# Big experts in fp32 on 64 and 32 wide column tiles, with 96 slots, one larger ring and experts in plain order

## The reference

```python
logits = (xf @ w_router).astype(jnp.float32)
vals, idx = lax.top_k(logits, TOP_K)
gates = jax.nn.softmax(vals, axis=-1)
combine = jnp.sum(jax.nn.one_hot(idx, N_EXPERTS, dtype=jnp.float32) * gates[..., None], axis=1)
for e in range(N_EXPERTS):
    y = y + combine[:, e:e + 1].astype(xf.dtype) * swiglu(xf, w1[e], w3[e], w2[e])
```

## Time and profile before

| what | value |
|---|---|
| median of 3 runs | 1207.49 us (1205.4 to 1207.52) |
| profiled execution, its own time | 1207.14 us |
| its span, first to last instruction | 1205.3 us |
| TensorE busy | 1149.9 us, 95% |
| VectorE busy | 669.2 us, 56% |
| ScalarE busy | 562.7 us, 47% |
| mean granted TensorE clock | 0.988 |
| moved | 351.08 MB, 291 GB/s over the span |
| weights split for big experts | 216 units on ScalarE (265.3 us) and on VectorE (308.0 us) |

### The profile page before, as it was taken

One profiled execution on the slowest core, in us unless ns is written; L12 is line 12 of the kernel. 1 busy time (PEld: TensorE's weight loads), 2 busy tenths in 40 slices (PEclk: granted clock), 3 DMA queues, 4 the chain that ended last, 5 costly groups with the idle time before them and its releaser, 6 DMA issues.

```text
span 1205.3 us, 16293 instructions
## 1 busy us (share of the span) xinstructions
PE 1149.9 (95%) x6555; PEld 852.7 (71%) x6555; DVE 669.2 (56%) x740; ACT 562.7 (47%) x642; POOL 49.6 (4%) x93
## 2 busy tenths in 40 slices
PE   5989899999999999899999999999999999999995
PEld 5979778888879976685486688648658468387351
DVE  4875664544455523582384788427578058574143
ACT  4772355344444476452363677226447056263131
POOL 8010000000000022000000000000000000000000
PEclk9999999999999999999999999999999999999998
DMA  9632059755325822139999999999999999999992
GB/s 319 184 116 72 29 169 369 238 175 187 128 70 177 330 74 72 66 139 416 413 415 410 413 415 412 400 414 414 411 414 415 415 412 412 413 413 415 413 407 78
DMA packets 116737, 351.08 MB, mean 291 GB/s; under 512 B 8136, under 2 KB 55280, under 8 KB 116656
## 3 DMA queue, kind: packets, MB, share of 16 engines
q1 hardware_dynamic: 115552, 347.11, 74.8%
q0 software_dynamic: 1104, 2.86, 0.8%
HBM read 348.89 MB, written 1.05 MB: 290 GB/s over the span
## 4 chain that ended last, share of the span: by engine, by line
PE 88%; DVE 4%; ACT 2%; DMA 2%; POOL 2%; issue 1%; POOLq 0%; DVEq 0%; ACTq 0%
PE ps L620 20%; PE ps L621 19%; PE ps L622 19%; PE ps L1717 11%; PE ps L1738 7%; PE ps L1661 3%; DMA room<-in_o_moe_w_dram 2%; PE ps L1673 1%; PE ps L1370 1%; DVE low L1904 1%; POOL level L741 1%; PE ps L1578 1%; PE ps L1590 1%; DMA gam<-in_e_sgu_w_dram 1%; PE ps L1698 1%
## 5 line engine op out<-in xcount | busy, mean ns | idle before, releaser
L1904 DVE TENSOR_TENSOR low<-room,all_hi 128x1408 fp32r<-128x1408 f32 (+1 forms) x216 | 308.0, 1458 | 202.6 <-ACT all_hi L883 202.0
L883 ACT ACTIVATE all_hi<-room 128x1408 fp32r<-128x1408 f32 (+1 forms) x216 | 265.3, 1255 | 258.6 <-DMA room<-in_o_moe_w_dram 177.4
L1717 PE MATMUL ps<-room,xg_raw 128*64 128x512 f32 (+1 forms) x768 | 152.5, 558 | 0.0
L620 PE MATMUL ps<-all_hi,xg_hi 128*128 128x512 f32 (+1 forms) x384 | 144.8, 377 | 2.0 <-DVE low L1904 1.0
L621 PE MATMUL ps<-low,xg_hi 128*128 128x512 f32 (+1 forms) x384 | 144.6, 376 | 0.0
L622 PE MATMUL ps<-all_hi,xg_lo 128*128 128x512 f32 (+1 forms) x384 | 144.0, 375 | 0.0
L620 PE MATMUL ps<-all_hi,x_hi 128*128 128x512 f32 (+1 forms) x336 | 125.1, 372 | 5.1 <-ACT xn L972 2.4
L621 PE MATMUL ps<-dense_lo,x_hi 128*128 128x512 f32 (+1 forms) x336 | 122.8, 366 | 0.0
L622 PE MATMUL ps<-all_hi,x_lo 128*128 128x512 f32 (+1 forms) x336 | 122.5, 365 | 0.0
L1717 PEld LDWEIGHTS ps<-room,xg_raw 128*64 128x64 f32 x768 | 54.6, 137 | 95.5 <-issue 95.4
L1897 DVE TENSOR_TENSOR dense_lo<-slots_a,all_hi 128x2048 fp32r<-128x2048 f32 x40 | 91.4, 2290 | 47.5 <-ACT all_hi L876 47.5
(11 more groups left out here) (363 smaller groups left out, 1566.9 us busy)
## 6 DMA issues: line engine op xcount, KB each, us to landing
room<-in_o_moe_w_dram SPq DMA_DIRECT2D x256, 704.0 KB, 15.6
room<-in_o_moe_w_dram SPq DMA_DIRECT2D x80, 1024.0 KB, 18.2
slots_c<-in_e_ffn_w_dram SPq DMA_DIRECT2D x36, 512.0 KB, 6.8
slots_a<-in_e_ffn_w_dram SPq DMA_DIRECT2D x30, 512.0 KB, 5.3
slots_a<-in_e_w_in_dram SPq DMA_DIRECT2D x24, 512.0 KB, 8.7
slots_a<-in_o_w_qkv_dram SPq DMA_DIRECT2D x18, 512.0 KB, 4.5
room<-in_o_moe_w_dram SPq DMA_DIRECT2D x16, 512.0 KB, 17.1
slots_a<-in_e_w_out_dram SPq DMA_DIRECT2D x8, 512.0 KB, 4.0
```

The costliest lines, as they stand in the source:

```text
L620: pe.matmul(o, a_hi, b_hi, start=first, stop=False)
L883: act.activation(unit_hi(st), raw_of(v, off, st.size), ACT.Copy).then_inc(hi_done, 1)
L1717: last = mm(ps[a * SMALL:(a + 1) * SMALL, o + b, 0:n], xg_raw[:, c, :], raw[a][:, c0:c0 + n], start=(c == 0), stop=(c == DC - 1))
L1904: tt(unit_lo(st), raw_of(v, off, st.size), unit_hi(st).bitcast(F32), ALU.subtract).then_inc(lo_done, 1)
```

## The change

1. Big experts no longer split their weights. Their products are plain fp32, with 96 slots instead of 128. The first 64 slots are done on two column tiles of 64, each with a quarter (704 columns, in two parts of 352) of the inner width. The remaining 32 slots are done on four column tiles of 32, with 384, 320, 384 and 320 columns. The down step does the same with 2 x 512 and 4 x 256 columns.
2. The slots lie in more places than before, so the turn, the way back (a second matrix `back_r`), the carrying back (`carry_back`) and the table of remainders (limits of 96, and 128 more behind them) follow the new layout. A remainder would now begin above 96 tokens.
3. The high parts of the dense weights and 11 KB behind the dense ring join the expert ring, which has 147 KB a partition. The two pieces of an up step pair of a big expert share a semaphore.
4. The phases run in plain order: (0, half 0), (0, half 1), (1), (2, half 0), ... The last expert's down phase writes bank 3, not bank 6.
5. ScalarE and VectorE keep the evacuations, SiLU, gate and additions. `xg_lo` and `m_lo` go.

```diff
@@ -41,9 +41,10 @@
     FC = FF // P
     NE = o_router.shape[2]
     CW = 256
-    SLOTS, SMALL = P, 64
-    NB = SEQ // SLOTS
-    NK = NB * NE
+    SLOTS, SMALL, MANY = P, 64, 96
+    LATE = MANY - SMALL
+    NK = 2 * NE + NE // 2
+    assert MANY + SLOTS < SEQ <= MANY + 2 * SLOTS
...
@@ -103,13 +104,19 @@
 
 
     HALF, HB = FF // 2, FC // 2
-    UP_COLS = ((0, 512), (512, 512), (1024, HALF - 1024))
+    QUART, WIDE, NARROW = HALF // 2, 384, 320
+    PAIR_COLS = ((0, 512), (512, 512), (1024, HALF - 1024))
+    MANY_COLS = ((0, QUART // 2), (QUART // 2, QUART // 2), (QUART, WIDE))
+    LATE_COLS = ((0, WIDE), (WIDE, NARROW), (QUART, WIDE), (QUART + WIDE, NARROW))
+    EVEN_BLOCKS = QUART // P
+    M64, M32 = HB * SMALL, (HB + 1) * LATE
+    assert QUART == WIDE + NARROW and QUART - EVEN_BLOCKS * P == SMALL and WIDE == 3 * P and HB == 2 * EVEN_BLOCKS + 1
...
         return q % 2 == 0
 
-    PHASE = [(0, 0), (1, 0), (0, 1)] + [(q, a) for q in range(2, NE) for a in range(2 if big(q) else 1)]
-    ENDING = [1, 0] + list(range(2, NE))
+    PHASE = [(q, a) for q in range(NE) for a in range(2 if big(q) else 1)]
+    ENDING = list(range(NE))
     PHASES = len(PHASE)
     LAST = [max(n for n in range(PHASES) if PHASE[n][0] == q) for q in range(NE)]
...
+            STEPS.append(st)
+
+
+    BEFORE, AFTER = 2 * SPLITS * DC * CW, 2 * HALF
+    ROOM = BEFORE + RING * DC * CW + AFTER
     ARRIVE = 20
...
+                    j, nb = pc.part
+                    both = o_moe_w2[0][bass.ds(e, 1), rows, :].rearrange("e (s r) d -> (e s) r d", s=2)
+                    r0 = j // 2 * P
+                    dst = raw_of(v, 0, pc.size)
+                    if nb == 2:
+                        src = both[:, r0:r0 + P, :].rearrange("s p d -> p s d")
+                        dst = dst.rearrange("p (s d) -> p s d", s=2)
+                    else:
+                        src = both[:, r0:r0 + SMALL, :]
...
-                n = SLOTS if big(q) else SMALL
+                n = MANY if big(q) else SMALL
                 pe.wait_ge(prep_done, TILES * (q + 1))
                 for c in range(DC):
                     for t in range(TILES):
...
                         pe.wait_ge(hTl_ready, TURN0 + 1)
-                    for i, j in enumerate(turn_blocks(b)):
-                        last = pe.transpose(ps[:, turn_bank(n, b), i * P:(i + 1) * P], u_act[:, j * P:(j + 1) * P], ident[:, :])
+                    o = ps[:, turn_bank(n, b), :]
+                    if not big(PHASE[n][0]):
+                        for i, j in enumerate(turn_blocks(b)):
+                            last = pe.transpose(o[:, i * P:(i + 1) * P], u_act[:, j * P:(j + 1) * P], ident[:, :])
+                    elif b == 0:
+                        for i in range(4):
+                            last = pe.transpose(o[:, i * P:(i + 1) * P], u_act[:, i * P:(i + 1) * P], ident[:, :])
+                    elif b == 1:
+                        pe.transpose(o[:, 0:P], u_act[:, 4 * P:5 * P], ident[:, :])
+                        for k in range(2):
+                            half = slice(k * SMALL, (k + 1) * SMALL)
+                            last = mm(o[half, P:P + SMALL], u_act[:, 5 * P:QUART], ident[:, half], start=True, stop=True)
+                    else:
+                        for i in range(3):
+                            pe.transpose(o[:, i * P:(i + 1) * P], u_act[:, QUART + i * P:QUART + (i + 1) * P], ident[:, :])
+                        at = 2 * P + LATE
+                        last = mm(o[SMALL:P, at:at + LATE], u_act[:, QUART + 2 * P:QUART + NARROW], ident[:, 3 * LATE:P],
+                                  start=True, stop=True)
                     last.then_inc(hT_done, 1)
 
...
                     last = pe.transpose(ps[0:SLOTS, bank, t * P:(t + 1) * P], sel_w[:, t, :], ident[:, :])
+                if big(q):
+                    for t in range(TILES):
+                        last = pe.transpose(ps[0:SLOTS, bank, SEQ + t * P:SEQ + (t + 1) * P], sel_r[:, t, :], ident[:, :])
                 last.then_inc(back_done, 1)
+
+            def carry_back(q, t):
+
+                for turn, cols, first in ((back, slice(0, 512), True), (back_r, slice(512, D), False)):
+                    for y in (y_hi, y_lo):
+                        for hf in range(2):
+                            rows = slice(hf * SMALL, (hf + 1) * SMALL)
+                            last = mm(ps[:, SCAT[q][2 * t + hf], :], turn[rows, t, :], y[rows, cols], start=first and y is y_hi,
+                                      stop=not first and y is y_lo)
+                            if not first and y is y_lo:
+                                last.then_inc(scat_done, 1)
 
             def scatter(q, parts=range(4)):
                 k = NTH[q]
...
                 turn = back_last if q == NE - 1 else back
+                if big(q):
+                    for t in sorted({m // 2 for m in parts}):
+                        carry_back(q, t)
+                    return
                 for m in parts:
                     if not big(q) and q < NE - 1 and m:
                         pe.wait_ge(scat_added, 4 * (k - 1) + m)
                     t, hf = m // 2, m % 2
-                    if big(q):
-                        for y, first in ((y_hi, True), (y_lo, False)):
-                            last = mm(ps[:, SCAT[q][m], :], turn[:, t, :], y[:, hf * 512:(hf + 1) * 512], start=first, stop=not first)
-                    else:
-                        rows = slice(hf * SMALL, (hf + 1) * SMALL)
-                        last = mm(ps[:, SCAT[q][m], :], turn[rows, t, :].bitcast(F32), y_small[rows, :], start=True, stop=True)
-                    last.then_inc(scat_done, 1)
+                    rows = slice(hf * SMALL, (hf + 1) * SMALL)
+                    mm(ps[:, SCAT[q][m], :], turn[rows, t, :].bitcast(F32), y_small[rows, :], start=True, stop=True)\
+                        .then_inc(scat_done, 1)
+
+            def arrived(st):
+
+                v, _ = st.pieces[-1]
+                pe.wait_ge(ring_in[arrive_sem(v)], arrive_count(v))
 
...
 
                 (c, w), o = st.part, 3 * st.part[1]
-                if st.big:
-                    pe.wait_ge(lo_done, A_MOE + st.at + 1)
-                    hi, lo = unit_hi(st), unit_lo(st)
-                    for b, (c0, n) in enumerate(UP_COLS):
-                        last = product(pe, ps[:, o + b, 0:n], xg_hi[:, c, :], xg_lo[:, c, :], hi[:, c0:c0 + n], lo[:, c0:c0 + n],
-                                       c == 0, c == DC - 1)
-                    last.then_inc(piece_used, 1)
-                    return
-                for v, _ in st.pieces:
-                    pe.wait_ge(ring_in[arrive_sem(v)], arrive_count(v))
+                first, end = c == 0, c == DC - 1
+                arrived(st)
                 raw = [raw_of(v, 0, HALF) for v, _ in st.pieces]
-                for b, (c0, n) in enumerate(UP_COLS):
-                    for a in range(2):
-                        last = mm(ps[a * SMALL:(a + 1) * SMALL, o + b, 0:n], xg_raw[:, c, :], raw[a][:, c0:c0 + n],
-                                  start=(c == 0), stop=(c == DC - 1))
+                if big(st.q):
+                    for b, (c0, n) in enumerate(MANY_COLS[0:2]):
+                        for a in range(2):
+                            mm(ps[a * SMALL:(a + 1) * SMALL, o + b, 0:n], xg_many[:, c, 0:SMALL],
+                               raw[0][:, a * QUART + c0:a * QUART + c0 + n], start=first, stop=end)
+                    for a, (c0, n) in enumerate(LATE_COLS):
+                        last = mm(ps[a * LATE:(a + 1) * LATE, o + 2, 0:n], xg_many[:, c, SMALL:MANY], raw[0][:, c0:c0 + n],
+                                  start=first, stop=end)
+                else:
+                    for b, (c0, n) in enumerate(PAIR_COLS):
+                        for a in range(2):
+                            last = mm(ps[a * SMALL:(a + 1) * SMALL, o + b, 0:n], xg_few[:, c, :], raw[a][:, c0:c0 + n],
+                                      start=first, stop=end)
                 last.then_inc(raw_used, 1)
 
             def down_step(st):
 
-                j = st.part
+                j, (v, off) = st.part, st.pieces[0]
                 first, end = st.a == 0 and j == 0, st.a == 1 and j == HB - 1
-                if st.big:
-                    pe.wait_ge(lo_done, A_MOE + st.at + 1)
-                    hi, lo = unit_hi(st), unit_lo(st)
-                    for hf in range(2):
-                        cs = slice(hf * 512, (hf + 1) * 512)
-                        last = product(pe, ps[:, 6 + hf, :], m_hi[st.n % 2][:, j, :], m_lo[st.n % 2][:, j, :], hi[:, cs], lo[:, cs],
-                                       first, end)
-                    last.then_inc(piece_used, 1)
-                    return
-                (v, off), = st.pieces
-                pe.wait_ge(ring_in[arrive_sem(v)], arrive_count(v))
+                arrived(st)
                 raw = raw_of(v, off, D)
```

(48 more changed lines are left out.)

315 lines of the change are left out of this document (125 added, 190 removed).

## The result

The changed kernel takes 1294.63 us (median, 1293.68 to 1295.96) against 1207.51 us beside it on the same chip: ratio 1.0725, 95% interval 1.0707 to 1.0744. The forecast was 1215 with a range of 1183 to 1264, so the result lies 80 us above the forecast and 31 above the range. The profiled execution has a span of 1293.5 us, 88.2 more than before. TensorE's first gather begins at 511.88 us, no later than before, so all of it lies in the expert part.

What follows compares the result with a forecast made beforehand. It took TensorE's summed steps to bound the kernel, transfers just keeping up. Up steps +6.4, down steps +3.5, other TensorE work +7.1 and vanishing waits -9.6 gave +7.4 us on 1207.14: 1215 us, range 1183 to 1264.

Steps and rivals of the forecast that it cites:

- the bare step: New big up step on TensorE without changes of tile width: 1.18 plus 0.645, about 1.83 us, against 1.929 before.
- rival 3: Big steps: only two 32-wide tiles run at once, +120 us, 1335 us for the kernel; chance 0.10.
- bare down step: New big down step without changes of width: 0.86 plus 0.43, together 1.29 us, against 1.387 before.
- the stalls and the small terms: TensorE outside the big steps: turns, gathers and way back add 7.1 us; stalls and waits that go save 9.6.
- The stall of the first pair: First down step, 2.20 us late at 596.39, then slow matmuls; forecast to go, saving 3.6 us.
- the wait before the last expert's down phase: TensorE's wait from 1160.60 to 1162.86; forecast to go through a separate bank, saving 2.3 us, plus 1.7 for its slow start.
- The turn: Transposes between up and down steps of a big half: some 1.8 us each, +0.6 x 8 halves = +4.8 us.
- the two changes of width: Each big step goes from 64-wide to 32-wide tiles and back: 0.084 plus 0.058, 0.142 us a step.
- the one gap at 860.71: Kernel before, entry from full array into 64-wide tiles: first tiled matmul starts 0.26 us after the last, 0.08 exposed.
- rival 1: Big steps: changes of width are free, 31 us less, 1184 us; chance 0.27 with what lies near it.
- rival 2: Big steps: the pipeline drains at each change of width, 0.36 us a step, +47 us, 1262 us; chance 0.18.
- the earlier transfers have nothing late to pay: Weight queue: at 413 GB/s with ample lead, transfers save nothing beyond the 3.6 us already counted and do not bound.

Runs made afterwards that it cites:

- e1_spread: The changed kernel with the last w2 block of each big half issued as two transfers of 64 rows instead of one: 1238.66 us, ratio 1.0257.
- e2_before_two_engines: The kernel before with only the last w2 block of each big half issued in the new form, outermost dimension 2: 1323.14 us, ratio 1.0948.

## Why the prediction was wrong, by its own steps

**Right: the bare step.** 704 x 1.68 = 1.18 us for the pair and 0.645 for the four 32-wide tiles were forecast; the blocks give 1.18 and 0.65. Four tiles of 32 do run at once, on four streams of weights (the four first instructions of the block at 519.67 start within 0.02 us), so rival 3 falls. 1.29 for a bare down step stands too (0.86 and 0.43 inside 1.01 and 0.57). So does the reading that TensorE's steps set the end as long as transfers come in time: e1_spread is 31.6 us above before by spans, and the steps' difference is 128 x 0.18 + 88 x 0.19 = 40 us, less 8.6 for the rest.

**Right in direction, 6 us off in size: the stalls and the small terms.** They were put at +7.1 and -9.6, -2.5 together; e1_spread leaves -8.6. The stall of the first pair and the wait before the last expert's down phase are gone, as forecast, and gathers take 3.72 to 3.77. The turn takes 1.57 us from 591.99 to 593.56, not 1.8: +3.0 instead of +4.8. Of the other 4 us of gain, 3 lie outside TensorE's steps, in two places that the prediction didn't look at: in e1_spread the first gather starts at 512.11 instead of 513.37, and between the last addition into h and the final norm lie 0.1 us (1229.15 to 1229.23) instead of 2.0 (1195.53 to 1197.57).

**Mis-sized: the two changes of width, 0.142 us a step.** They cost 0.16 + 0.12 = 0.28, twice that, which makes (0.28 - 0.142) x 216 = 30 us. The value came from the one gap at 860.71 and an argument on weight loads. The nearer rows were in the prediction and not used for this: a block of 4 instructions has 0.15 us over its slope (its time less what its instructions take at the rate of one more in a long block), which is what a 64-wide block pays to be entered. Two entries at 0.15 give 0.30. The forecast used that intercept as part of the price of a round trip, for the high bound only (0.34). It should have been the value taken, since each new step is two such blocks. Neither rival 1 (free) nor rival 2 (0.36, a whole drain) holds; the price lies outside the forecast's own 0.08 to 0.22 and nearer to rival 2 than to 0.142. The Trainium skill's rule on the change of tiling mode (TensorEngine Tiling (Array Packing), Key Properties) had been weighed down because of that same gap. The instructions' start-to-start times show a cost near it, 0.28 where a whole drain would be 0.37.

**Wrong: "the earlier transfers have nothing late to pay".** This is the step that took the result out of the range: 56 us. It took 413 GB/s from the kernel before for all transfers after, and so costed the bytes and the lead but not the shape of each new transfer. In its place the runs showed eight transfers on two engines each: the one between 1127 and 1174 us lost 12 us of queue time, and of such losses TensorE's time paid 7.1 us a transfer on average. The prediction also named the test for this, waits of TensorE in the small up phases, and these came: 21.8 us at L1728. Of the 56 us, the longer small up phases are 4.7 + 10.9 + 12.9 = 28.5 us, against 37.84. The three stops before the last block are 6.40 + 6.43 + 7.83 = 20.7 us beyond a normal 0.57. That leaves 7 us, and the slow clock behind each stop, with a further short wait of 0.3 us, accounts for it: the three blocks from 853.97 take 1.90, 1.39 and 2.16 us instead of 1.01, 0.57 and 1.34, which is 2.5 us; the other two stops have 2.4 and 2.6.

**What could have been seen.** The rows of before had no price for such a transfer, but a bound could be worked out from 413 GB/s and the diff: with two of sixteen engines 10.2 us of queue time eight times, 71 us beyond the 1.3 that each takes on all, and 1286 us for the kernel. That case had no place among the rivals. Beside that of two tiles at once (1335) it would have been the only one beyond the range, and the nearest to the result. Even so it would not have been the right size: in the kernel with a full queue the eight cost 113 us, and in the changed one 56.

**What the right direction owes.** Slower was forecast with 0.59, from +7.4 us. Without the transfer it would have come out slower by 31 us, through changes of width that cost twice the value taken, and still inside the stated range. With it, most of the 87 us comes from a term that the sum put at nothing.

## What to carry to other kernels

Read each new transfer's shape as well as its bytes: an outermost dimension of 2 turned 512 KB into 12 to 14 us of lost queue time, and TensorE paid a part of it in the changed kernel and all of it in the one whose queue was full. When a step alternates between forms of an instruction, price each block by what a short block takes beyond its instructions at the rate of a long one, and order the work so that blocks of one form meet; that alone took off 22 us here, and the three remedies together turned a kernel 7% slower into one 1.3% faster.

## What the runs showed of the hardware that I had not expected

- A transfer with an outermost dimension of 2 moved 49 GB/s for 8 us, 0.12 of the 411 beside it. SyncE's next issue took 8.75 us meanwhile (8.0 to 9.9 behind each of the eight in e2_before_two_engines), and after it the queue moved about 290 GB/s for 17 us with all engines busy (e2, 714 to 731 us).
- Two transfers of 256 KB onto 64 partitions each moved about 260 GB/s at a full share of busy engines, where one of 512 KB onto 128 partitions moved 413; 3.7 us lost each time.
- A change from 32-wide to 64-wide column tiles costs 0.16 us and one back 0.12 us (by single starts at 518 to 521 us: before a change the next start comes 0.10 us later than the rate of the block gives, and after it the second start comes 0.05 later in 64-wide blocks and 0.02 in 32-wide ones), though the records of neighbours overlap (1.40 us long, next start after 1.34).
- Four column tiles of 32 stream fp32 at the rate of one, 0.65 us for 384 columns each. Extra matmuls of 64 columns in such a block cost nothing (1239.29 against 1238.66 us).
